# A decoder step with a 32-expert mixture: one more place for weights, bias products in four corners, and the first experts' rows gathered two experts at a time

## The reference

```python
a = rms_norm(h, g_mix); h = h + mixers(a) @ w_out      # gated linear recurrences, two groups of heads
xt = rms_norm(h, g_ffn)
logits = xt @ w_router + b_router                       # 32 experts
top_v, top_i = top_k(logits, 4); gates = softmax(top_v)
for each chosen expert e of a token:
    gate, up = split(x @ w_gu[e] + b_gu[e])             # 1024 -> 2 x 1024
    gate = min(gate, 7); up = clip(up, -7, 7)
    hid = (up + 1) * (gate * sigmoid(1.702 * gate))
    h += gates * (hid @ w_dn[e] + b_dn[e])              # 1024 -> 1024
h = h + sigmoid(rms_norm(h, g_ple) @ w_ple_gate) * (p @ w_ple_proj)
y = rms_norm(h, g_final)
```

## Time and profile before

| what | us |
|---|---|
| median of 3 runs | 1227.04 (1226.78 to 1228.18) |
| the profiled execution, its own time | 1228.99 |
| its span, first to last instruction | 1227.2 |
| PE busy | 1174.7 (96%) |
| DVE busy | 278.0 (23%) |
| ACT busy | 183.1 (15%) |
| POOL busy | 22.9 (2%) |
| moved by the DMA queues | 437.68 MB, mean 357 GB/s |

### The profile page before, as it was taken

The page is one execution under the profiler, slowest core; times in us unless marked ns, Lnnn a source line. Parts: engine busy times, 40 slices in busy tenths (PEclk is TensorE's granted clock), DMA queues, the critical chain, the costliest instruction groups (busy, mean ns, idle before and its releaser), DMA issues.

```text
span 1227.2 us, 12765 instructions
## 1 busy us (share of the span) xinstructions
PE 1174.7 (96%) x5466; PEld 565.9 (46%) x5467; DVE 278.0 (23%) x508; ACT 183.1 (15%) x314; POOL 22.9 (2%) x45
## 2 busy tenths in 40 slices
PE   9999999999999999999999999999999999989997
PEld 6767776544344444443333333333333344333365
DVE  3165832211121121112111211121112111111144
ACT  3151141211011010111010101010101111111032
POOL 4002000000000000000000000000000000000000
PEclk9999999999999999999999999999999999999998
DMA  9552589679999999999999999999999999999941
GB/s 226 139 140 82 147 268 420 250 304 418 416 407 417 416 417 417 417 417 417 417 418 417 417 417 416 418 417 418 416 418 418 417 417 417 417 417 417 413 168 40
DMA packets 125777, 437.68 MB, mean 357 GB/s; under 512 B 9740, under 2 KB 58008, under 8 KB 92920
## 3 DMA queue, kind: packets, MB, share of 16 engines
q1 hardware_dynamic: 122144, 434.02, 89.4%
q10 hardware_dynamic: 3304, 2.55, 0.8%
q0 software_dynamic: 272, 0.28, 0.1%
HBM read 432.08 MB, written 4.72 MB: 356 GB/s over the span
## 4 chain that ended last, share of the span: by engine, by line
PE 55%; DMA 40%; DVE 2%; ACT 2%; issue 1%; SPq 0%; ACTq 0%; DVEq 0%
PE ps L904 52%; DMA ring<-in_w_dn 37%; DMA vmask<-in_w_dn 2%; PE ps L1334 1%; PE ps L1346 1%; DMA tok<-in_x_prompt 0%; ACT wst L818 0%; DVE ring L1531 0%; DVE acc L1476 0%; SPq L565 0%; DVE tok L1479 0%; PE ps L921 0%; DVE ring L1616 0%; DVE ring L1541 0%; DVE wst L1842 0%
## 5 line engine op out<-in xcount | busy, mean ns | idle before, releaser
L904 PE MATMUL ps<-ring,wst 128*64 128x512 f32 x888 | 209.3, 600 | 27.6 <-DMA ring<-in_w_dn 26.9
L904 PE MATMUL ps<-ring,aT 128*64 128x512 f32 x952 | 208.2, 592 | 0.8 <-ACT aT L811 0.8
L904 PE MATMUL ps<-ring,s 128*64 128x512 f32 x840 | 187.1, 593 | 1.9 <-DMA ring<-in_w_gu 1.9
L904 PEld LDWEIGHTS ps<-ring,wst 128*64 128x64 f32 x888 | 58.7, 136 | 169.7 <-issue 100.3
L1771 DVE TENSOR_SCALAR wst<-ps 128x512 f32<-128x512 f32 x32 | 22.1, 692 | 499.5 <-PE ps L904 499.5
L904 PEld LDWEIGHTS ps<-ring,aT 128*64 128x64 f32 x952 | 68.1, 137 | 135.7 <-issue 135.7
L904 PEld LDWEIGHTS ps<-ring,s 128*64 128x64 f32 x840 | 59.8, 137 | 123.5 <-issue 115.3
L904 PE MATMUL ps<-aT,wst 128*128 128x288 f32 x384 | 97.0, 413 | 3.0 <-ACT ring L730 3.0
L830 ACT ACTIVATE wst<-wst 128x512 f32<-128x512 f32 x32 | 20.2, 630 | 502.7 <-DVE wst L1771 502.7
L904 PE MATMUL ps<-sel,tok 128*128 128x256 f32 x384 | 93.0, 381 | 0.0
L904 PEld LDWEIGHTS ps<-aT,wst 128*128 128x128 f32 x384 | 73.3, 193 | 24.6 <-ACT ring L730 3.4
(11 more groups left out here) (265 smaller groups left out, 753.8 us busy)
## 6 DMA issues: line engine op xcount, KB each, us to landing
ring<-in_w_gu SPq DMA_DIRECT2D x224, 1024.0 KB, 20.9
ring<-in_w_dn SPq DMA_DIRECT2D x111, 1024.0 KB, 24.1
vmask<-in_w_gu SPq DMA_DIRECT2D x17, 1024.0 KB, 20.4
wst<-in_w_in SPq DMA_DIRECT2D x28, 512.0 KB, 3.8
acc<-in_w_gu SPq DMA_DIRECT2D x12, 1024.0 KB, 20.0
vmask<-in_w_dn SPq DMA_DIRECT2D x11, 1024.0 KB, 24.1
acc<-in_w_dn SPq DMA_DIRECT2D x6, 1024.0 KB, 21.9
ring<-in_w_ple_gate SPq DMA_DIRECT2D x4, 1024.0 KB, 18.5
```

The lines of the kernel that those rows point to most:

```text
L904: return pe.matmul(o, lhsT, rhs, start=start, stop=stop, skip_group_check=True)
```

## The change

- The tiles that only the stages ahead of the experts need (`smp`, `smask`, `maski`, `vec_rows`, `lbt`, `r1w`, `r1T`, `gk2`, `dec`) are cut from one tile `misc` of 8 KB on a partition. `misc` is a place that is used over and over, `M_SLOT`, ninth in `FIRST`. So 18 units are filled ahead and 15 places are reused, where 17 and 14 were. The room comes from `bgu`, which becomes narrower.
- `bgu` holds the gate biases in rows 0 to 31 and the up biases in rows 64 to 95, loaded by two transfers of POOL instead of one. `ehot` has a one in row e and in row 64 + e (`pick` is made once by DVE). The four products of `bias` take 64 rows each: two for rows 0 to 63 into bank 0, two for rows 64 to 127 into bank 1.
- The rows of group 0 are gathered for experts 0 and 1 first (128 columns for each product), then for experts 2 and 3 by `gather_second`, four chunks after expert 0 and four at the end of expert 1. Three chunks, not two, go ahead of expert 0's first product. DVE's selection is split in the same way. The rows of group 1, one pair of chunks in each of experts 0 to 3 before, come as two pairs in expert 2 and two in expert 3; `select(1)` moves from expert 0 to expert 2. Later groups are as before.

The diff, cut to its core:

```diff
-smp = sb("smp", [P, 2, P])
-smask = sb("smask", [P, SB])
+misc = sb("misc", [P, UCOLS])
...
+def front_only(n):
+    v = misc[:, misc_at[0]:misc_at[0] + n]
+    misc_at[0] += n
+    assert misc_at[0] <= UCOLS
+    return v
+smp = front_only(2 * P).rearrange("p (i k) -> p i k", i=2)
+smask = front_only(SB)
...
-maski = sb("maski", [P, P + 32], I32)
+maski = front_only(P + 32).bitcast(I32)
...
-vec_rows = sb("vec_rows", [NV, P])
+vec_rows = front_only(P)[0:NV]
...
+lbt = front_only(6 * HH).rearrange("p (i h) -> p i h", i=6)
+r1w = front_only(KD * 32).rearrange("p (c r) -> p c r", c=KD)
+r1T = front_only(T)
+gk2 = front_only(GH * GK)
+dec = front_only(KU * (NCH + SB)).rearrange("p (u n) -> p u n", u=KU)
...
-bgu = sb("bgu", [P, 2 * FF])
+bgu = sb("bgu", [P, D + T])
...
+pick = sb("pick", [P, E])
...
+HALF_Q = QUAD // 2
+def gathered(g, j):
+    return j + 1 if g == 0 else QUAD * g + 2 + j + 1
+def sel_made(g):
+    return NT + 1 + g
...
-V_SLOT, A_SLOT, S_ONCE, H_ONCE, Y_ONCE = range(UNITS, UNITS + 5)
-place_loaded = u_loaded + [state_loaded[0], w_loaded[0], w_loaded[1]]
-earlier_loads = {8: 1, V_SLOT: 1, S_ONCE: 1, H_ONCE: NG + 1, Y_ONCE: NG + 1}
-FIRST = (6, 7, 9, 10, 11, 0, S_ONCE, H_ONCE, 1, 2, 3, 4, 5, V_SLOT, Y_ONCE, 8, A_SLOT)
+slots.insert(UNITS + 2, misc[:])
+V_SLOT, A_SLOT, M_SLOT, S_ONCE, H_ONCE, Y_ONCE = range(UNITS, UNITS + 6)
+place_loaded = u_loaded + [r1w_loaded, state_loaded[0], w_loaded[0], w_loaded[1]]
+earlier_loads = {8: 1, V_SLOT: 1, M_SLOT: 5, S_ONCE: 1, H_ONCE: NG + 1, Y_ONCE: NG + 1}
+FIRST = (6, 7, 9, 10, 11, 0, S_ONCE, H_ONCE, M_SLOT, 1, 2, 3, 4, 5, V_SLOT, Y_ONCE, 8, A_SLOT)
...
-    if i <= A_SLOT:
+    if i <= M_SLOT:
         queue.append((i, u))
...
-            sp.wait_ge(bgu_loaded, 16)
+            sp.wait_ge(bgu_loaded, 32)
...
-    pool.dma_start(bgu[0:E, :], io["b_gu"][0]).then_inc(bgu_loaded, 16)
+    pool.dma_start(bgu[0:E, 0:FF], io["b_gu"][0][:, 0:FF]).then_inc(bgu_loaded, 16)
+    pool.dma_start(bgu[SLOTS:SLOTS + E, 0:FF], io["b_gu"][0][:, FF:2 * FF]).then_inc(bgu_loaded, 16)
...
     def copy_gathered(g, j):
-        act.wait_ge(xg_done, QUAD * g + j + 1)
+        act.wait_ge(xg_done, gathered(g, j))
+        n = HALF_Q if g == 0 else QUAD
         bank = XG_BANK[j] if g == 0 else 2
-        act.copy(xsT[g % 2][:, 2 * j:2 * j + 2].rearrange("p c x s -> p (c x s)"), ps[:, bank, :]).then_inc(xs_copied, 1)
+        act.copy(xsT[g % 2][:, 2 * j:2 * j + 2, 0:n, :], ps[:, bank, 0:2 * n * SLOTS].rearrange("p (c x s) -> p c x s", c=2, x=n)) \
+            .then_inc(xs_copied, 1)
+    def copy_second(i):
+        act.wait_ge(xg_done, QUAD + i + 1)
+        act.copy(xsT[0][:, 4 * i:4 * i + 4, HALF_Q:QUAD, :], ps[:, 2, :].rearrange("p (c x s) -> p c x s", c=4, x=HALF_Q)) \
+            .then_inc(xs_copied, 1)
...
         act.copy(hidT, ps[:, 3, :]).then_inc(hT_copied, 1)
-        if e + QUAD < E:
+        if e == 0:
+            copy_second(0)
+        if e in (2, 3):
+            for j in range(2):
+                copy_gathered(1, 2 * (e - 2) + j)
+        if e >= QUAD and e + QUAD < E:
             copy_gathered(e // QUAD + 1, e % QUAD)
         if e % 2 == 1:
             act.wait_ge(st_done, e // 2 + 1)
             act.copy(selT[:], ps[:, 3, 0:T]).then_inc(st_copied, 1)
+        if e == 1:
+            copy_second(1)
...
+    def add_bias():
+        for b in range(2):
+            r = slice(b * SLOTS, (b + 1) * SLOTS)
+            for half in range(2):
+                mm(ps[half * SLOTS:(half + 1) * SLOTS, b, :], ehot[r], bgu[r, half * BANK:(half + 1) * BANK],
+                   True, False)
...
     def bias(e):
         pe.wait_ge(ehot_ready, e + 1)
         if e == 1:
             pe.wait_ge(gateT_copied, 1)
-        for b in range(2):
-            halves(b, ehot[:], bgu[:, b * FF:b * FF + BANK], bgu[:, b * FF + BANK:(b + 1) * FF], True, False)
+        add_bias()
...
-                pe.wait_ge(xs_copied, QUAD * g + j)
+                pe.wait_ge(xs_copied, gathered(g, j) - 1)
             if j == 0 and g:
-                pe.wait_ge(sel_ready, g + NT)
+                pe.wait_ge(sel_ready, sel_made(g))
             if j == 1 and g == 0:
                 pe.wait_ge(cnt_ready, 1)
         bank = XG_BANK[j] if g == 0 else 2
-        w = QUAD * SLOTS
+        n = HALF_Q if g == 0 else QUAD
+        w = n * SLOTS
         for t in range(NT):
             if g == 0 and c == 0:
                 pe.wait_ge(sel_ready, t + 1)
             ins = mm(ps[:, bank, (c % 2) * w:(c % 2 + 1) * w], tok[:, t, c * P:(c + 1) * P],
-                     sel[:, t].rearrange("p x s -> p (x s)"), t == 0, t == NT - 1)
+                     sel[:, t, 0:n].rearrange("p x s -> p (x s)"), t == 0, t == NT - 1)
         if c % 2 == 1:
             ins.then_inc(xg_done, 1)
+    def gather_second(i):
+        pe.wait_ge(sel_ready, NT + 1)
+        pe.wait_ge(xs_copied, QUAD + i)
+        w = HALF_Q * SLOTS
+        for c in range(4):
+            for t in range(NT):
+                ins = mm(ps[:, 2, c * w:(c + 1) * w], tok[:, t, (4 * i + c) * P:(4 * i + c + 1) * P],
+                         sel[:, t, HALF_Q:QUAD].rearrange("p x s -> p (x s)"), t == 0, t == NT - 1)
+        ins.then_inc(xg_done, 1)
...
-            pe.wait_ge(xs_copied, e + c // 2 + 1)
+            pe.wait_ge(xs_copied, gathered(e // QUAD, c // 2))
+        if e == HALF_Q and c == 0:
+            pe.wait_ge(xs_copied, QUAD + 2)
...
-    for c in range(2):
+    for c in range(3):
         gather_chunk(0, c)
...
-                for k in (2, 3) if c == 0 else (4, 5) if c == 1 else (6, 7):
+                for k in (3,) if c == 0 else (4, 5) if c == 1 else (6, 7):
                     gather_chunk(0, k)
...
         if e == 0:
-            for k in range(2):
-                gather_chunk(1, k)
+            gather_second(0)
         pe.wait_ge(hid_ready, e + 1)
...
-        if e and g + 1 < E // QUAD:
-            gather_chunk(g + 1, 2 * j)
+        if e < QUAD:
+            ahead, later = ((), (), (0, 1), (4, 5))[e], ((), (), (2, 3), (6, 7))[e]
+        elif g + 1 < E // QUAD:
+            ahead, later = (2 * j,), (2 * j + 1,)
+        else:
+            ahead, later = (), ()
+        for c in ahead:
+            gather_chunk(g + 1, c)
         if e >= 2:
             combine_half(e // 2 - 1, e % 2)
-        if e and g + 1 < E // QUAD:
-            gather_chunk(g + 1, 2 * j + 1)
+        for c in later:
+            gather_chunk(g + 1, c)
         if e % 2 == 1:
             pe.wait_ge(selg_ready, g + 1)
             pe.wait_ge(hT_copied, e + 1)
@@ -1346,6 +1409,8 @@
                 ins = pe.transpose(ps[:, 3, t0:t0 + m], selg[0:m, t, j - 1:j + 1, :].rearrange("p a s -> p (a s)"),
                                    ident[0:m, 0:m])
             ins.then_inc(st_done, 1)
+        if e == 1:
+            gather_second(1)
...
+        dve.tensor_copy(ehot[:], pick[:, e:e + 1].to_broadcast([P, SLOTS])).then_inc(ehot_ready, 1)
+    lk.add(dve.tensor_tensor(pick[:], ident[:, 0:E], ident[:, SLOTS:SLOTS + E], ALU.add))
+    lk.wait()
     hot(0)
...
     for t in range(NT):
-        dve.tensor_tensor(sel[:, t], iota1[:, 0:SLOTS].unsqueeze(1).to_broadcast([P, QUAD, SLOTS]),
-                          rankp[:, t, 0:QUAD].unsqueeze(2).to_broadcast([P, QUAD, SLOTS]),
+        dve.tensor_tensor(sel[:, t, 0:HALF_Q], iota1[:, 0:SLOTS].unsqueeze(1).to_broadcast([P, HALF_Q, SLOTS]),
+                          rankp[:, t, 0:HALF_Q].unsqueeze(2).to_broadcast([P, HALF_Q, SLOTS]),
                           ALU.is_equal).then_inc(sel_ready, 1)
...
+    dve.tensor_tensor(sel[:, :, HALF_Q:QUAD], iota1[:, 0:SLOTS].unsqueeze(1).unsqueeze(1).to_broadcast([P, NT, HALF_Q, SLOTS]),
+                      rankp[:, :, HALF_Q:QUAD].unsqueeze(3).to_broadcast([P, NT, HALF_Q, SLOTS]),
+                      ALU.is_equal).then_inc(sel_ready, 1)
...
+            dve.wait_ge(sel_ready, sel_made(g))
...
-            if e + QUAD < E:
-                dve.wait_ge(selg_ready, g + 1)
-                dve.wait_ge(xg_done, QUAD * (g + 1))
-                select(g + 1)
+        if e == HALF_Q or e >= QUAD and e % QUAD == 0 and e + QUAD < E:
+            g = e // QUAD
+            dve.wait_ge(selg_ready, g + 1)
+            dve.wait_ge(xg_done, gathered(g, QUAD - 1) if g else QUAD + 2)
+            select(g + 1)
```

More of the change, by code:

```diff
@@ L165, in build @@
         smp_tmp = acc[:, GH:KD, :].rearrange("p c t -> p (c t)")[:, 0:SB * P].rearrange("p (b v) -> p b v", b=SB)
-        smp = sb("smp", [P, 2, P])
-        smask = sb("smask", [P, SB])
+        misc = sb("misc", [P, UCOLS])
+        misc_at = [0]
+        def front_only(n):
[5 more added lines that the diff above has]
+        smask = front_only(SB)
         squares = tok[:].rearrange("p t d -> p (t d)")[:, 0:KD * T].rearrange("p (c t) -> p c t", t=T)
@@ L193, in build @@
         V_GN = V_LB + 2 * HH
-        lbt = sb("lbt", [P, 6, HH])
-        r1w = sb("r1w", [P, KD, 32])
-        r1T = sb("r1T", [P, T])
-        gk2 = sb("gk2", [P, GH * GK])
```

(21 more changed lines are left out.)

## The result

| | before | after |
|---|---|---|
| median of 19 executions each, us | 1228.30 (1226.71 to 1229.31) | 1223.87 (1222.63 to 1226.87) |
| ratio | | 0.997 (95% interval 0.9963 to 0.9976) |
| the profiled execution, its own time and span | 1228.99, 1227.2 | 1222.63, 1220.8 |
| PE, DVE, ACT busy | 1174.7, 278.0, 183.1 | 1155.8, 278.3, 183.5 |

A forecast was written before the change was run, and what follows sets the result against it. The DMA's weight stream, full from about expert 4's first request, was taken as the bound: -3.9 (earlier request), -2.5 (one unit fewer) and -0.3 (restart) make -6.7 us, off the 1227.04 median 1220.4; range 1217.2 to 1225.0.

The forecast's parts named there:

- The corners overlap: Against a rival in the bias products: row halves don't overlap, bias stays 1.77 us, +3.3, 1223.7; chance 0.10.
- the weight loads don't set the pace: Against a rival in half-width gathers: weight loads make them 0.19 a record, +6.7, no change at 1227.0; chance 0.06.
- The first-gap rival: PE isn't late in experts 2 and 3, so 7.1 us at expert 1's request count: -9.6, 1217.4; chance 0.08.
- The fifteenth place: Weight prefetch: 18 units filled ahead instead of 17, so one unit fewer remains behind any use; -2.5 us.
- First product of expert 0: Start of expert 0 after its first gathers: three smaller chunks go ahead of it and it comes 1.6 us earlier.
- Price of a half-width gather: Gathers of 128 columns on PE: 0.12 us a record, ends 0.11 and 0.19, against 0.233 for a full one.
- Bias: Four 64 x 64 corner products take 0.95 instead of 1.77 us; four before expert 4's first use give -3.3.
- No sum changes, but the cycles do: Group 1's 48 full gather records move to experts 2 and 3: total unchanged, expert 1's cycle 25.3 us.
- a wait in the new order: Rival: in experts 1 to 3, pairs sharing bank 2 await ACT's copy; 1 to 2 us, 1222; chance 0.08.
- Sum: Expert 4's first use: -1.6 + 1.0 - 3.3 = -3.9 us, so its request at 340.4 instead of 344.32.
- The restart: Weight stream restarting from empty at expert 4's request: -0.3 us between the losses on restarting.
- Start of the gathers: After bias(0): a shorter bias moves the ranks only up to memb's arrival; gathers begin at 221.9, -0.2 us.

The follow-up runs named there:

- bdn_later: Changed kernel with the eight b_dn products moved from the first pair's combination to that of experts 8 and 9; 1217.85 us, ratio 0.9914.
- bias0_twice: Changed kernel with bias(0)'s four products issued twice, the second set overwriting the same sums; 1224.88 us, ratio 0.9973.
- cover_wait: Changed kernel with gather_second(1), and ACT's copy of it, moved ahead of the selection's transposes in expert 1; 1222.07 us, ratio 0.9946.
- after_again: The changed kernel unaltered, measured again; 1224.14 us, ratio 0.997 to the kernel before.
- no_place: Changed kernel without the fifteenth place: 17 units filled ahead and 14 places reused, as before; 1226.25 us, ratio 0.9983.
- both_keep5: Changed kernel with expert 1's wait covered, b_dn's products in experts 8 and 9, and five instead of three identity products after bias(0); 1219.57 us, ratio 0.9928.
- place_bias_bdn: Kernel before plus the fifteenth place, the new bias and b_dn's products in experts 8 and 9, gathers unsplit; 1224.49 us, ratio 0.9977.
- wide_bias: Bias products over 128 rows again: on the changed kernel 1226.94 us (0.9986); with b_dn's products also in experts 8 and 9, 1220.93 us (0.9946).
- all_three: Changed kernel with expert 1's wait covered, b_dn's products in experts 8 and 9, and bias(0) issued twice; 1218.27 us, ratio 0.9914.
- experiment 12: The run both_keep5: five instead of three identity products after bias(0), with the wait covered and b_dn's products later; 1219.57 us, ratio 0.9928.

## Why the prediction was wrong, point by point

Its mechanism held. The stream is empty ahead of expert 4's request and full behind it (417 GB/s); PE's waits for `w_dn` rows in `ring` grew from 26.9 to 32.3 us (less than forecast); biases before the request count and the 27 after it don't; one place is worth one unit. The corners overlap, the weight loads don't set the pace, the corners don't run in series, PE isn't the bound: these rivals are out. The first-gap rival is out for this kernel, and it is exactly what `bdn_later` makes true.

Step by step:

- **The fifteenth place:** forecast -2.5, measured -2.1 between medians, -2.3 between executions at a clock of .994 or more. Right.
- **First product of expert 0:** forecast -1.6, measured 9.06 - 7.47 = 1.59. Right.
- **Price of a half-width gather:** 0.12 a record forecast; the batches of 24 records take 2.88 start to start (272.69 - 269.81), 0.12, and 2.78 in expert 0's tail (244.94 - 242.16). The batch of 6 costs 0.145 a record and those of 12 cost 0.128. Over group 0 that is 9.6 us behind the first product of expert 0 where 9.4 was forecast.
- **Bias:** 0.95 forecast, 1.02 measured, so -3.0 instead of -3.3. In `bias0_twice` a second set of four costs 0.85, so 0.17 of the 1.02 is getting in and out of the four corners. The Trainium skill (TensorEngine Tiling (Array Packing), Key Properties) has a drain at each change of tiling mode; the trace agrees in so far as there is such a price, and for the two changes here it is at most these 0.17 us. The estimate of 1.15 from the Trainium skill (TensorE: Matmul & The Clock Gate, Measured speedup vs the span model) was further off than the batch of 32 x 64 products.
- **"No sum changes, but the cycles do" (group 1 of the gathers), and with it the cycle of 25.3 for expert 1: the step that failed.** The cycle is 27.22, and 1.40 of the excess is PE waiting for ACT's copy, at a place where the moved pair had been the cover. The prediction named the cover of the hidden chain in expert 0 and did not ask for that of expert 1: the step counted what the moved pair costs where it goes, and not what it had hidden where it came from. `cover_wait` takes the wait away: its cycle is 25.43, the request comes 1.8 earlier and the time is 1.8 to 2.1 less. The rival "a wait in the new order" had a chance of 0.08; its size (1 to 2 us) and its range of experts (1 to 3) fit, but it looked for the wait at bank 2, between two pairs of gathers, where none came, and not at the transposes. By the prediction's own sign, a wait of PE in experts 1 to 3, it was wrong.
- **Sum:** expert 4's use -1.6 + 1.0 - 3.3 = -3.9 forecast; measured -1.66. The difference of 2.2 is the wait 1.4, the bias 0.3, the small batches 0.1 to 0.2, and some 0.4 in the steps from one batch to the next, more than half of it beside that wait.
- **The restart** was forecast at -0.3, and this term did better than that. Between the two requests 35 units are requested. Before, 88.61 us at 406 GB/s moved 34.3 of them, so 0.7 of a unit (1.7 us) was still to come at 344.32, and 0.9 was lost after it: 2.6. After, 51.53 us at 404 and 42.04 at 379 moved all 35, so nothing was left at 342.04, and 1.8 was lost after it. That is -0.8. The account is then -1.7 - 2.5 - 0.8 = -5.0. The medians of executions at the higher clock say 1223.63 against 1228.30, -4.7; the two profiled executions say -5.8 from bias(0) to the end of the stream, but before's is 0.7 over its median and after's 1.0 under that of its kind. A rate that is read as 417 over 820 us is uncertain by 1 us from its rounding alone, so the three agree as far as they can be read.
- **Start of the gathers:** -0.2 forecast for the shorter bias(0), -0.16 measured (bias(0) to the first gather 5.37 against 5.53). Not in the prediction: with the short first bias more of the executions seem to fall to half clock there. The place was seen in three of the profiled executions (`after_again`, `no_place`, `both_keep5`), of the others only the mean clock is known, and a fall can be too short for that to show it: `place_bias_bdn`'s profiled execution has a mean of .996. Over the study, 25 of 87 executions of kernels with the short first bias have a mean granted clock under .994, 8 of 101 of those with a long one (the kernel before, both `wide_bias` kernels, `bias0_twice`, `all_three`). The grouping was made with the data in hand, and a single pair of kernels is too small to show it: `wide_bias` against `after_again` is 1 against 5 of 12. Such an execution is mostly 2 to 5 us longer. In the kernel after they put the mean (1224.37) 0.7 over the median of the rest. The Trainium skill (TensorE: Matmul & The Clock Gate, What's actually happening) describes two levels of the clock, and the traces here agree (PEclk 1.00 and 0.50); why this change of under 1 us of work should make the lower one more frequent is not shown, and the remedy tried in experiment 12 failed.

So expert 4's request came 2.2 us short of the forecast, 1.4 of it a wait exposed by a moved cover, and the restart gave 0.5 back: 5.0 of the 6.7 remain by the account, 4.7 by the medians at the higher clock. The ratio's 3.7 is what the means differ by (1224.37 and 1228.10): the executions at a lower clock put the mean of the kernel after 0.7 over the median of the others, and the mean of the kernel before lies 0.2 under its median. That is the other 1.0.

## What to carry to other kernels

When work is moved, price both ends: what it costs where it goes, and which chain on another engine it had covered where it was. When products of two forms stand in turn, taking one kind out frees more than its own spacing: 3.4 us for four of 0.68 here. When a stream of transfers is starved at two places, an earlier request at the first is worth nothing until the second no longer runs empty: here the same split of the gathers was worth 0 with `b_dn`'s products in the first pair, and 6.6 us with them moved to where PE waits anyway, so look for the edit that makes an earlier one count. And forecast a difference against many executions of the kernel before, not against the profile or three times.

## What was not expected of the hardware

- Four float32 products of 512 columns on 64 x 64 corners take 1.02 us with both changes of form, 0.58 of the 1.77 of the same four on 128 x 64; four more right behind them take 0.85.
- A queue that ran empty restarts at 341 GB/s over 10 us when requests come 1.72 us apart; 10 us at the same point of the work move at 424 GB/s where it had not run empty (`bdn_later`, from 336).
- Four products of 128 x 128 form and 288 columns take 1.94 us in a row, and 5.34 in turn with four of 32 x 128 form, where each takes about 0.68.
- The granted clock can go to half though PE was idle for no longer than 1.2 us at a time just before, in some executions and not in others of the same kernel: it fell 0.1 us after the start of bias(0) in `place_bias_bdn`, 1.1 after it in `after_again`, and two more identity products behind bias(0) didn't prevent it (three of six executions of `both_keep5`).
